# First rows of a mixture of experts by one-hot products, and its first weights loaded during the projection before it

## The chip, the cores and the metric

The kernel runs on one core of a Trainium2 chip. Five engines share its SBUF: TensorE (PE) multiplies matrices into PSUM, VectorE (DVE) and ScalarE (ACT) work elementwise, GpSimd (POOL) works elementwise and issues the indirect DMAs, SyncE (SP) issues most of the others. Sixteen DMA engines move data between HBM and SBUF. The metric is the device time of one execution in microseconds.

## The reference, cut to what matters

One sequence of 512 tokens of width 1024, fp32. A first block (a recurrent branch, an attention branch, a projection) gives h1; a hierarchical mixture of experts is added to it; a second block of two layers follows. The change is in the mixture and just ahead of it:

```python
mix = (ga * y_a + gb * y_b) @ w_out[l]
h = h + g1[:, None, :] * mix                      # h1
u2 = modulate(h, norm2_g[l], sh2, sc2)
# hier_moe: 4 groups x 8 experts, the best group, its two best experts for each token
g_sel = jnp.argmax(g_logits, axis=-1)
e_top, e_loc = lax.top_k(e_logits, 2)
gate = g_w * jax.nn.softmax(e_top, axis=-1)
hid = jax.nn.silu(xb @ w1[e]) * (xb @ w3[e])      # for the rows of expert e, D_EXPERT = 512
ys  = hid @ w2[e]
out = segment_sum(ys * row_gate, row_tok)
```

512 tokens with two experts each make 1024 assignments over 32 experts.

## The kernel before

**Around the change.** The weights of the first block stream through `wring`, five slots of 1 MB. SP loads a slot when PE has left it (`w_used`, L1401). The last projection (`out`) uses four slots, with homes 0 to 3, and the router's weights the one after, with home 4. Each slot takes 16 x 3 matmuls of PE. DVE adds each of eight results to x, which gives h1 (`h1_rdy`), and PE, ACT and DVE make the router's logits. ACT writes the normed rows to `u_tok` in SBUF and stores them to HBM as `u_rows` (`u_stored`).

**Routing.** DVE works out for each token its two experts, then (`ohot`) PE counts: `pos` is a token's place within its expert. From that DVE computes where each token goes: `tixI` is an index into a table in HBM, `destI` the row of its result. Each expert has a block of 64 rows, two experts are a pair, so a pair has 128 rows: 16 pairs, with spare blocks behind an `If` that is not taken here. POOL scatters the token numbers into the table (8 indirect DMAs, L1494), reads it back as `ids`, and for each pair gathers 128 rows of `u_rows` into `xs` (L1484). Rows of the table to which no token belongs hold 0, so row 0 is gathered for them. For pair 0 alone a shorter way is there: DVE makes a selection matrix `big` (L2018: token by row, 1 where the token is the j-th of expert 0 or 1), PE multiplies it by the token numbers (L2310), and the result `ids0` serves the first gather at once.

**The pairs.** `mring` has 12 parts of 1 MB on the bytes of `wring` and behind: for each of the pair's two experts a = 0, 1, four parts of w1 and w3 and two of w2, at places 6a + j. They cover homes 0 to 4 of `wring` (places 0 to 4), so a part cannot be loaded before its bytes are free. SP issues them in the order of its loop (L1419 for w1 and w3, L1428 for w2): all of pair 0 but the last two parts after h1 is complete, and from then on each part when its predecessor has been used (`used13`, `used2`). PE, for each pair: `gate_up` of expert 0, `down` of the previous pair's expert 1, `gate_up` of expert 1, the turning of the next pair's rows (`turn_x`, L2319), `down` of expert 0. In the first two pairs it also turns h1 to token rows (`h1_rows_turned`). DVE adds the shift to the turned rows (`x_turned`, L2076), which `gate_up` waits for. Results are stored to `y_rows`, gathered from there by `destI` (L1507) and added to h1.

**On PE ahead of pair 0**: count products, L2310, then `turn_x(0)`, then eight small products for `gate_row` (L2385), then pair 0. **On DVE**: the routing chain up to `destI` (L2048), block counts, `route_rdy`, then `x_turned(0)` (when the gather has landed and been turned), the gates, `gate_row`.

Of the kernel before, what the change touches and what calls it, by code (L numbers as in the profile page):

```python
# [31 lines left out]
MOE_ROWS = 64  # L32
MOE_PAIRS = EXPERTS // 2
# [43 lines left out]
def home(slot):  # L77

    return (slot + 1) % SLOTS
# [79 lines left out]
def build(nc, xT, crow, wmod, wrest, wfirst, wlayers, consts, vectors, brow, frow, lamv, rpb, w13, w2, out):  # L159
# [16 lines left out]
    with ExitStack() as ctx:  # L176

        def at(name, kb, shape, dt=F32):
            return nc.alloc_sbuf_tensor_at(name, shape, dt, offset=(nc.sbuf_base + 31) // 32 * 32 + int(kb * 1024))
# [50 lines left out]
        zeros = at("zeros", 116.5, [P, MOE_ALL + 1], I32)  # L230
# [40 lines left out]
        ids0 = at("ids0", 158.25, [P, 1], I32)  # L271
# [88 lines left out]
        shift_sum, shift_kept, picked, ids0_full, ids0_rdy = (sem(n) for n in ("shift_sum", "shift_kept", "picked", "ids0_full", "ids0_rdy"))  # L360
# [1024 lines left out]
        def _(sp):  # L1385
# [28 lines left out]
            def part13(p, a, src):  # L1414

                for j in range(4):
                    if not (isinstance(p, int) and p == 0):
                        sp.wait_ge(used13[a], 4 * p + j - 3)
                    sp.dma_start(mring[:, 6 * a + j, :], src(j)).then_inc(part_in[6 * a + j], 16)  # L1419

            def part2(p, a, src):

                for j in range(2):
                    if not (isinstance(p, int) and p == 0):
                        sp.wait_ge(used2[a], 2 * p + j - 1)
                    elif 6 * a + 4 + j == router:
                        sp.wait_ge(A.free, A_ROWS + 1)
# [40 lines left out]
        def _(pool):  # L1468
# [4 lines left out]
            pool.memset(zeros[:], 0).then_inc(pool_step, 1)  # L1473
            pool.wait_ge(pool_step, 1)
            pool.dma_start(table.rearrange("(p b) o -> p (b o)", p=P), zeros[:]).then_inc(table_clear, 16)
# [5 lines left out]
            def gather(p, rows):  # L1481
                if p >= 1:
# [28 lines left out]
            for p in range(1, MOE_PAIRS):  # L1511
                gather(p, ids[:, p:p + 1])
# [247 lines left out]
        def _(dve):  # L1760
# [246 lines left out]
            def chosen(to, by):  # L2007
# [8 lines left out]
            step(STT(out=q0, in0=b[:, 0:NQB * EXPERTS].rearrange("p (s e) -> p s e", e=EXPERTS)[:, :, 0:2], scalar=1.0, in1=M[:, :, 0:2], op0=ALU.add, op1=ALU.mult))  # L2016
            pick = big[:].rearrange("p (s a j) -> p s a j", s=NQB, a=2)
            TT(pick, K("block")[:, 1:].unsqueeze(1).unsqueeze(1).broadcast_to((P, NQB, 2, MOE_ROWS)),  # L2018
               q0.unsqueeze(3).broadcast_to((P, NQB, 2, MOE_ROWS)), ALU.is_equal).then_inc(picked, 1)
# [28 lines left out]
            step(dve.tensor_copy(destI[:], T("blk8")))  # L2048
            bb = big[:].rearrange("p (b e) -> p b e", e=EXPERTS)
# [22 lines left out]

            def x_turned(p):

                dve.wait_ge(xt_full, p + 1)
                dve.tensor_tensor(xT_[:], ps[:, 0:2, :].rearrange("p a (c n) -> p (a c) n", n=P),  # L2076
                                  mod[:, 24:32].unsqueeze(2).broadcast_to((P, DC, P)), ALU.add).then_inc(xt_done, 1)
# [46 lines left out]
            x_turned(0)  # L2124
# [60 lines left out]
        def _(pe):  # L2185
# [116 lines left out]

            pe.wait_ge(ohot, 1)
# [5 lines left out]
            for r in range(NQB):  # L2309
                ins = pe.matmul(ps[:, 7, 0:1], big[:, r * P:(r + 1) * P], K("token")[:, r:r + 1], start=(r == 0), stop=(r == NQB - 1))  # L2310
            ins.then_inc(ids0_full, 1)
            pe.wait_ge(A.free, A.made)
            pe.wait_ge(B.free, B.made)

            def turn_x(p):

                pe.wait_ge(xs_in, 16 * p + 16)
# [63 lines left out]
            turn_x(0)  # L2381
            pe.wait_ge(ids0_rdy, 1)
            for n in range(2):
                for c in range(4):
                    ins = pe.matmul(ps[n * 64:(n + 1) * 64, 7, c * P:(c + 1) * P], mod[:, 40 + 4 * n + c:41 + 4 * n + c].broadcast_to((P, 64)), ident,  # L2385
                                    start=True, stop=True)
            ins.then_inc(h1_turned, 1)
# [226 lines left out]
```

## Time and profile before

| what | value |
|---|---|
| median of 3 runs | 3367.93 us (3364.71 to 3369.0) |
| the profiled execution | 3363.76 us, span 3361.9 us |
| granted TensorE clock, mean | 0.973 of full |
| PE busy | 3045.0 us, 91% of the span |
| DVE, ACT, POOL busy | 1536.4, 988.9, 942.7 us |
| DMA | 465.80 MB, mean 139 GB/s |
| expert stage (first weight issue to last product) | about 641 to 1182 us |

Times in the trace are from the start of the span. The page divides the span into 40 slices of 84 us. A row of a timeline is a start, a duration (for merged instructions, of all of them), an engine, a line of the kernel, and in brackets how long the engine had been idle and what ended it. PEclk 1.00 is 2.4 GHz and 0.50 is 1.2 GHz. An fp32 matmul that is no transpose shows as two records.

### The profile page before, as it was taken

The page shows a single profiled execution, that of the slowest core. Times are in us where ns is not written, and L with a number is a line of the kernel's source. Part 1 is how long each engine was busy: PE and PEld are TensorE (multiplying, and loading weights), DVE is VectorE, ACT ScalarE, POOL GpSimd, SP SyncE. Part 2 cuts the span into 40 slices and gives each one's busy share as a digit, 9 for nine tenths or more (in the row PEclk, how much of TensorE's full clock was granted, in tenths as well). Part 3 has the DMA queues.
Part 4 walks back from the last instruction along what each step waited for, and adds up shares of the span by engine and source line. Part 5 has one row for each costly group of instructions (what it writes and reads, how often), then busy time and mean ns, then how long its engine had stood idle before and what let it go on. Part 6 is the DMA issues. An engine that isn't in the chain of part 4 may idle for free.

```text
span 3361.9 us, 32946 instructions
## 1 busy us (share of the span) xinstructions
PE 3045.0 (91%) x13112; PEld 2082.9 (62%) x13112; DVE 1536.4 (46%) x2562; ACT 988.9 (29%) x1398; POOL 942.7 (28%) x346
## 2 busy tenths in 40 slices
PE   3999998787777769999998899999999999889998
PEld 2777655632222247776745688887676755578886
DVE  7598856421111133645556622231645455742233
ACT  3653233200000043325243322223423434232222
POOL 2243102110000034332221344445432311244432
PEclk9999999999999979999999899999999999989999
DMA  5236312499999942121211122222121121122221
GB/s 226 88 113 239 112 50 80 168 367 422 422 422 422 421 156 74 67 76 52 87 50 38 63 100 100 90 99 95 50 88 63 63 75 38 50 76 93 95 100 50
DMA packets 71229, 465.80 MB, mean 139 GB/s; under 512 B 8785, under 2 KB 9073, under 8 KB 18993
## 3 DMA queue, kind: packets, MB, share of 16 engines
q1 hardware_dynamic: 60192, 436.31, 33.7%
q0 software_dynamic: 5200, 17.07, 1.4%
q10 hardware_dynamic: 5696, 10.49, 0.8%
q8 instruction: 95, 1.56, 0.2%
q14 instruction: 46, 0.37, 0.0%
HBM read 451.24 MB, written 12.60 MB: 138 GB/s over the span
## 4 chain that ended last, share of the span: by engine, by line
PE 75%; DMA 12%; DVE 8%; ACT 2%; issue 1%; POOL 0%; SPq 0%; ACTq 0%; DVEq 0%; POOLq 0%
PE ps L438 15%; PE ps L439 14%; PE ps L440 14%; DMA mring<-w 10%; PE ps L745 3%; PE ps L728 3%; PE ps L730 2%; PE ps L729 2%; PE ps L427 2%; PE ps L2256 2%; PE ps L908 2%; PE ps L760 1%; PE ps L2330 1%; PE ps L1014 1%; PE ps L973 1%
## 5 line engine op out<-in xcount | busy, mean ns | idle before, releaser
L497 POOL TENSOR_TENSOR w_lo<-wring,w_hi 128x2048 fp32r<-128x2048 f32 (+1 forms) x198 | 813.7, 4116 | 1729.6 <-ACT w_hi L487 1729.5
L438 PE MATMUL ps<-x_hi,w_hi 128*128 128x512 f32 (+1 forms) x1480 | 587.9, 397 | 18.2 <-ACT ps L1593 7.8
L440 PE MATMUL ps<-x_hi,w_lo 128*128 128x512 f32 (+1 forms) x1480 | 578.2, 391 | 0.0
L487 ACT ACTIVATE w_hi<-wring 128x2048 fp32r<-128x2048 f32 x176 | 336.0, 1911 | 315.9 <-PE ps L438 292.3
L439 PE MATMUL ps<-xf_lo,w_hi 128*128 128x512 f32 x1080 | 422.2, 391 | 0.0
L438 PEld LDWEIGHTS ps<-x_hi,w_hi 128*128 128x128 f32 (+1 forms) x1480 | 278.6, 188 | 90.4 <-ACT ps L1593 8.2
L440 PEld LDWEIGHTS ps<-x_hi,w_lo 128*128 128x128 f32 (+1 forms) x1480 | 278.5, 188 | 59.2
L2330 PE MATMUL ps<-mring,xT__95 128*64 128x512 f32 x512 | 242.6, 606 | 58.6 <-DMA mring<-w 54.6
L2331 PE MATMUL ps<-mring,xT__95 128*64 128x512 f32 x512 | 242.8, 606 | 0.0
L439 PEld LDWEIGHTS ps<-xf_lo,w_hi 128*128 128x128 f32 x1080 | 204.1, 189 | 41.7
L1368 DVE TENSOR_TENSOR g_f<-ps,g_f 128x512 f32<-128x512 f32 x44 | 30.4, 692 | 366.5 <-PE ps L440 350.0
L2330 PEld LDWEIGHTS ps<-mring,xT__95 128*64 128x64 f32 x512 | 63.9, 137 | 188.5 <-DMA mring<-w 123.8
L728 PE MATMUL ps<-x_hi,w_hi 128*128 128x512 f32 x336 | 159.0, 473 | 0.0
L1700 ACT ACTIVATE sil<-ps 64x512 f32<-64x512 f32 x32 | 19.0, 595 | 472.3 <-PE ps L2331 472.3
L2083 DVE TENSOR_TENSOR hid<-ps,sil 64x512 f32<-64x512 f32 x32 | 21.8, 682 | 296.3 <-ACT sil L1700 296.3
L439 PE MATMUL ps<-xa_lo,w_hi 128*128 128x512 f32 (+1 forms) x400 | 156.0, 390 | 0.0
L2349 PE MATMUL ps<-mring,hidT 128*64 128x512 f32 x512 | 116.9, 598 | 42.7 <-DVE hidT L2088 42.7
L1484 POOL DMA_INDIRECT xs<-u_rows,ids x16 | 15.2, 951 | 461.9 <-PE ps L2319 405.8
L438 PE MATMUL ps<-g_hi,w_hi 128*128 128x512 f32 x352 | 137.7, 391 | 0.0
L440 PE MATMUL ps<-g_hi,w_lo 128*128 128x512 f32 x352 | 137.0, 389 | 0.0
L439 PE MATMUL ps<-g_lo,w_hi 128*128 128x512 f32 x352 | 137.0, 389 | 0.0
L730 PE MATMUL ps<-x_hi,w_lo 128*128 128x512 f32 x336 | 132.7, 395 | 0.0
(520 smaller groups left out, 5468.1 us busy)
## 6 DMA issues: line engine op xcount, KB each, us to landing
mring<-w SPq DMA_DIRECT2D x192, 1024.0 KB, 28.4
wring<-wlayers SPq DMA_DIRECT2D x148, 1024.0 KB, 4.7
wring<-wfirst SPq DMA_DIRECT2D x44, 1024.0 KB, 4.8
mods<-wrest SPq DMA_DIRECT2D x16, 1024.0 KB, 4.7
wmodS<-wmod SPq DMA_DIRECT2D x4, 2048.0 KB, 18.2
y_rows<-ysb ACTq DMA_DIRECT2D x64, 128.0 KB, 6.5
rp<-rpb POOLq DMA_DIRECT2D x16, 192.0 KB, 2.6
hT<-xT SPq DMA_DIRECT2D x1, 2048.0 KB, 18.1
```

Of the source, the lines that this page charges most:

```text
L427: ins = pe.matmul(bank, w[:, 0:m], rhs[:, k, :], start=(k == 0), stop=(k == nk - 1))
L438: said(pe.matmul(bank, wh[:, 0:m], hi[:, k, :], start=(k == 0), stop=False))
L439: pe.matmul(bank, wh[:, 0:m], lo[:, k, :], start=False, stop=False)
L440: ins = pe.matmul(bank, wl[:, 0:m], hi[:, k, :], start=False, stop=(k == nk - 1))
L487: act.activation(w_hi[:, q % HI_SLOTS, :], wring[:, home(g), :], ACT.Copy).then_inc(hi_rdy, 1)
L497: ins = pool.tensor_tensor(w_lo[:, home(slot), o:o + n], wring[:, home(slot), o:o + n], w_hi[:, q % HI_SLOTS, o:o + n].bitcast(F32), ALU.s ...
L728: said(pe.matmul(state["bank"], wh, x[0][:, k, :], start=(k == 0), stop=False))
L730: ins = pe.matmul(state["bank"], wl, x[0][:, k, :], start=False, stop=(k == DC - 1))
L745: ins = pe.matmul(ps[:, 4 + k % 2, 0:u["nk"] * P], u["q"], u["k"], start=True, stop=True)
L2330: pe.matmul(ps[MOE_ROWS:P, 2 + a, :], x, w[:, 0:SEQ], start=(k == 0), stop=(k == DC - 1))
L2331: ins = pe.matmul(ps[0:MOE_ROWS, 2 + a, :], x, w[:, SEQ:D], start=(k == 0), stop=(k == DC - 1))
L2349: ins = pe.matmul(ps[n * MOE_ROWS:(n + 1) * MOE_ROWS, 5 + a, :], hidT[:, a, k, :], w[:, n * SEQ:(n + 1) * SEQ], start=(k == 0), stop=(k == 3))
```

## The change

1. Pair 0's rows are no longer gathered. PE multiplies `u_tok` by the selection matrix `big`, eight chunks by four token blocks, straight into the banks that `turn_x` writes; DVE's `x_turned(0)` follows right behind `destI`.
2. A second selection matrix, `big1`, gives pair 1's token numbers (`ids1`), with which the first gather is issued. It takes the place of `ids0`. Pairs 2 to 15 use `ids` as before.
3. The table is cleared to 2^20 in place of 0, and gathers have a bounds check, so that places without a token are skipped. Pair 1's `ids1` holds 0 for them.
4. SP issues parts (1,2) and (1,3) when the mix is complete, and (0,0), (0,1), (0,2) as PE leaves the slots of `out`. When h1 is complete it issues the other seven, (1,4) and (1,5) among them, which came behind the first reissues before.
5. The `gate_row` products move ahead of the count products on PE.

```diff
+            def first(a, j):
+                src = w13[a, j] if j < 4 else w2[a, j - 4]
+                sp.dma_start(mring[:, 6 * a + j, :], src).then_inc(part_in[6 * a + j], 16)
             assert router == 4
+            sp.wait_ge(mix2_rdy, DC)
+            first(1, 2)
+            first(1, 3)
+            for j in range(3):
+                slot = one["out"] // CHUNKS + j
+                sp.wait_ge(w_used, slot + 1)
+                first(0, j)
             sp.wait_ge(h1_rdy, DC)
-            for p in range(MOE_PAIRS):
+            for a, j in ((0, 3), (1, 0), (1, 1), (0, 5), (1, 4), (1, 5)):
+                first(a, j)
+            sp.wait_ge(A.free, A_ROWS + 1)
+            first(0, 4)
+            for p in range(1, MOE_PAIRS):
                 part13(p, 0, lambda j, e=2 * p: w13[e, j])
-                if p >= 1:
+                if p >= 2:
                     part2(p - 1, 1, lambda j, e=2 * p - 1: w2[e, j])
...
-            pool.memset(zeros[:], 0).then_inc(pool_step, 1)
+            pool.memset(none[:], NO_ROW).then_inc(pool_step, 1)
...
-                pool.indirect_dma_start(xs[:], None, u_rows, bass.IndirectOffsetOnAxis(ap=rows, axis=0)).then_inc(xs_in, 16)
+                pool.indirect_dma_start(xs[:], None, u_rows, bass.IndirectOffsetOnAxis(ap=rows, axis=0),
+                                        bounds_check=SEQ - 1, oob_is_err=False).then_inc(xs_in, 16)
-            pool.wait_ge(ids0_rdy, 1)
+            pool.wait_ge(ids1_rdy, 1)
             pool.wait_ge(u_stored, 16 * NQB)
-            gather(0, ids0[:, 0:1])
+            gather(1, ids1[:, 0:1])
...
+            pick(big, 0)
+            dve.wait_ge(picked, 1)
+            pick(big1, 1)
...
-            dve.wait_ge(ids0_full, 1)
-            dve.tensor_copy(ids0[:], ps[:, 7, 0:1]).then_inc(ids0_rdy, 1)
             whole(T("nb"), cts, MOE_ROWS, EXPERTS)
+            dve.wait_ge(ids1_full, 1)
+            dve.tensor_copy(ids1[:], ps[:, 6, 0:1]).then_inc(ids1_rdy, 1)
...
             step(dve.tensor_copy(destI[:], T("blk8")))
+            x_turned(0)
...
+            for n in range(2):
+                for c in range(4):
+                    ins = pe.matmul(ps[n * 64:(n + 1) * 64, 7, c * P:(c + 1) * P], ...)
+            ins.then_inc(h1_turned, 1)
             pe.wait_ge(ohot, 1)
...
             pe.wait_ge(picked, 1)
-            for r in range(NQB):
-                ins = pe.matmul(ps[:, 7, 0:1], big[:, r * P:(r + 1) * P], K("token")[:, r:r + 1], start=(r == 0), stop=(r == NQB - 1))
-            ins.then_inc(ids0_full, 1)
             pe.wait_ge(A.free, A.made)
+            for c in range(DC):
+                for r in range(NQB):
+                    ins = pe.matmul(ps[:, c // 4, (c % 4) * P:(c % 4 + 1) * P], u_tok[:, r, c * P:(c + 1) * P], big[:, r * P:(r + 1) * P],
+                                    start=(r == 0), stop=(r == NQB - 1))
+                if c == 1:
+                    pe.wait_ge(picked, 2)
+                    for r in range(NQB):
+                        row = pe.matmul(ps[:, 6, 0:1], big1[:, r * P:(r + 1) * P], K("token")[:, r:r + 1], start=(r == 0), stop=(r == NQB - 1))
+                    row.then_inc(ids1_full, 1)
+            ins.then_inc(xt_full, 1)
...
-            turn_x(0)
-            pe.wait_ge(ids0_rdy, 1)
```

## Rows read from the trace of the kernel before

**Rows 1.** The page, the 40 slices: what the DMA moved.

```profile
GB/s 226 88 113 239 112 50 80 168 367 422 422 422 422 421 156 74 67 76 52 87 50 38 63 100 100 90 99 95 50 88 63 63 75 38 50 76 93 95 100 50
```

**Rows 2.** Windows: length, busy time of the engines, PEclk, DMA share, GB/s.

```profile
606.00:640.00 34.00, 34.00 (x151) 27.93 (x149) 13.59 (x15) 10.42 (x15) 4.62 (x1) 1.00 0.00 0
641.00:672.00 31.00, 13.88 (x80) 8.96 (x76) 19.35 (x86) 10.59 (x15) 1.47 (x2) 0.75 0.98 394
672.00:684.00 12.00, 8.28 (x43) 6.63 (x45) 2.92 (x9) 1.59 (x3) 8.00 (x9) 0.66 0.28 87
684.00:1173.00 489.00, 383.04 (x1764) 129.54 (x1760) 74.65 (x116) 19.02 (x32) 14.72 (x16) 0.99 1.01 421
```

**Rows 3.** The chain that ended last: start, us, what.

```profile
655.20 14.20 DMA u_rows<-u_tok
...
688.83 12.05 DMA xs<-u_rows,ids
...
816.11 30.24 DMA mring<-w
```

**Rows 4.** Timeline of POOL, four gathers of one pair each.

```profile
731.07 0.94 POOL L1484 DMA_INDIRECT xs<-u_rows,ids  x1 [26.92 <-PE ps L2319]
757.73 0.94 POOL L1484 DMA_INDIRECT xs<-u_rows,ids  x1 [25.71 <-PE ps L2319]
...
817.27 0.94 POOL L1484 DMA_INDIRECT xs<-u_rows,ids  x1 [31.57 <-PE ps L2319]
849.63 0.94 POOL L1484 DMA_INDIRECT xs<-u_rows,ids  x1 [31.42 <-PE ps L2319]
```

**Rows 5.** Timeline of SP's queue, 560 to 700 us.

```profile
564.58 32.60 SPq L1401 DMA_DIRECT2D wring<-wfirst  x4
641.00 4.26 SPq L1419 DMA_DIRECT2D mring<-w  x8
...
682.74 4.86 SPq L1419 DMA_DIRECT2D mring<-w  x4
687.64 0.95 SPq L1428 DMA_DIRECT2D mring<-w  x2
```

**Rows 6.** Timeline of PE ahead of pair 0.

```profile
655.42 0.49 PE L2305 MATMUL ps<-gt,cs 128*128 128x128 f32 x2 [1.21 <-DVE gt L1994]
...
657.34 1.05 PE L2310 MATMUL ps<-cs,big 128*128 128x1 f32 x8 [1.06 <-DVE big L2018]
675.72 1.94 PE L2319 MATMUL ps<-cs,xs 128*128 128x128 f32 x8 [17.33 <-DMA xs<-u_rows,ids]
677.59 2.66 PE L2385 MATMUL ps<-cs,small 128*64 128x128 f32 x15
679.84 0.76 PE L2331 MATMUL ps<-mring,xT__95 128*64 128x512 f32 x1
```

**Rows 7.** Timeline of DVE, selection, destI and x_turned.

```profile
656.39 0.17 DVE L2016 SCALAR_TENSOR_TENSOR gt<-ps,gt 128x8 f32<-128x8 f32 x1
656.59 0.69 DVE L2018 TENSOR_TENSOR big<-cs,gt 128x512 f32<-128x512 f32 x1
...
665.21 0.17 DVE L2048 CAST destI<-gt 128x8 int32<-128x8 f32 x1
...
677.70 1.22 DVE L2076 TENSOR_TENSOR xT__95<-ps,small 128x1024 f32<-128x1024 f32 x1 [10.07 <-PE ps L2319]
```

**Rows 8.** Instructions of L2310: ns min/median/max, first and last start.

```profile
L2310 PEld LDWEIGHTS ps<-cs,big x8: 186/192/192, 657.3 to 658.1; 128*128 128x128 f32 x8
```

**Rows 9.** Windows of 1 us; PEclk is the third number from the end.

```profile
650.00:651.00 1.00, 0.98 (x5) 0.58 (x4) 0.86 (x5) 0.86 (x2) 0.00 (x0) 0.50 1.03 434
653.00:654.00 1.00, 0.83 (x8) 0.56 (x6) 0.90 (x5) 0.60 (x2) 0.00 (x0) 1.00 0.88 303
659.00:660.00 1.00, 0.00 (x0) 0.00 (x0) 0.83 (x5) 0.00 (x0) 0.00 (x0) 0.81 1.03 434
```

**Rows 10.** The chain that ended last, end of the expert stage.

```profile
1177.95 3.68 PE ps L2349 x16
```

More of the change, by code:

```diff
@@ L32 @@
 MOE_ROWS = 64
+NO_ROW = 1 << 20
 MOE_PAIRS = EXPERTS // 2
@@ L229, in build @@
         browS = sm(GROUPS + EXPERTS)[0:1, :]
-        zeros = at("zeros", 116.5, [P, MOE_ALL + 1], I32)
+        none = at("none", 116.5, [P, MOE_ALL + 1], I32)
         xr = at("xr", 96, [P, RC, SEQ + CONV_W])
@@ L270, in build @@
         ids = at("ids", 158, [P, MOE_ALL + 1], I32)
-        ids0 = at("ids0", 158.25, [P, 1], I32)
+        ids1 = at("ids1", 158.25, [P, 1], I32)
+        big1 = at("big1", 150, [P, NQB * P])
         shift_e = at("shift_e", 170.25, [P, 1])
@@ L1416, in part13 @@
                 for j in range(4):
-                    if not (isinstance(p, int) and p == 0):
-                        sp.wait_ge(used13[a], 4 * p + j - 3)
+                    sp.wait_ge(used13[a], 4 * p + j - 3)
                     sp.dma_start(mring[:, 6 * a + j, :], src(j)).then_inc(part_in[6 * a + j], 16)
@@ L1423, in part2 @@
                 for j in range(2):
[L1424 to L1427, printed above, removed]
+                    sp.wait_ge(used2[a], 2 * p + j - 1)
                     sp.dma_start(mring[:, 6 * a + 4 + j, :], src(j)).then_inc(part_in[6 * a + 4 + j], 16)
+            def first(a, j):
+                src = w13[a, j] if j < 4 else w2[a, j - 4]
+                sp.dma_start(mring[:, 6 * a + j, :], src).then_inc(part_in[6 * a + j], 16)
             assert router == 4
-            sp.wait_ge(h1_rdy, DC)
-            for p in range(MOE_PAIRS):
+            sp.wait_ge(mix2_rdy, DC)
[3 more added lines that the diff above has]
+                slot = one["out"] // CHUNKS + j
+                assert home(slot) == j
+                sp.wait_ge(w_used, slot + 1)
+                first(0, j)
+            sp.wait_ge(h1_rdy, DC)
+            for a, j in ((0, 3), (1, 0), (1, 1), (0, 5), (1, 4), (1, 5)):
[3 more added lines that the diff above has]
+            for p in range(1, MOE_PAIRS):
                 part13(p, 0, lambda j, e=2 * p: w13[e, j])
-                if p >= 1:
+                if p >= 2:
                     part2(p - 1, 1, lambda j, e=2 * p - 1: w2[e, j])
@@ L1472, in _ @@
             pool.memset(xr[:, :, 0:CONV_W - 1], 0.0).then_inc(pad_rdy, 1)
-            pool.memset(zeros[:], 0).then_inc(pool_step, 1)
+            pool.memset(none[:], NO_ROW).then_inc(pool_step, 1)
             pool.wait_ge(pool_step, 1)
-            pool.dma_start(table.rearrange("(p b) o -> p (b o)", p=P), zeros[:]).then_inc(table_clear, 16)
+            pool.dma_start(table.rearrange("(p b) o -> p (b o)", p=P), none[:]).then_inc(table_clear, 16)
             pool.dma_start(browS, brow).then_inc(brow_in, 16)
@@ L1510, in _ @@
             pool.dma_start(final_row[:], frow.partition_broadcast(P)).then_inc(row_in, 16)
-            for p in range(1, MOE_PAIRS):
+            for p in range(2, MOE_PAIRS):
                 gather(p, ids[:, p:p + 1])
@@ L2048, in _, with x_turned @@
             step(dve.tensor_copy(destI[:], T("blk8")))
+            def x_turned(p):
+                dve.wait_ge(xt_full, p + 1)
+                dve.tensor_tensor(xT_[:], ps[:, 0:2, :].rearrange("p a (c n) -> p (a c) n", n=P),
+                                  mod[:, 24:32].unsqueeze(2).broadcast_to((P, DC, P)), ALU.add).then_inc(xt_done, 1)
+            x_turned(0)
             bb = big[:].rearrange("p (b e) -> p b e", e=EXPERTS)
@@ L2122, in pair_dve @@
                     gated_out(p, 1)
-            x_turned(0)
             gates()
@@ L2301, in _ @@
                         rows_turned(r, n)
+            for n in range(2):
+                for c in range(4):
+                    ins = pe.matmul(ps[n * 64:(n + 1) * 64, 7, c * P:(c + 1) * P], mod[:, 40 + 4 * n + c:41 + 4 * n + c].broadcast_to((P, 64)), ident,
+                                    start=True, stop=True)
+            ins.then_inc(h1_turned, 1)
             pe.wait_ge(ohot, 1)
@@ L2379, in pair_pe @@
                     down(p, 1)
-            turn_x(0)
-            pe.wait_ge(ids0_rdy, 1)
[L2383 to L2387, printed above, removed]
             for p in range(2):
```

19 lines of the change are left out of this document (8 added, 11 removed).

## The prediction

> **What bounds the kernel now.** I read the page's forty slices first: in six neighbouring slices the DMA moves 421 to 422 GB/s, which nothing else in the kernel approaches [rows 1]. That is the expert stage. The windows give it exactly: over 684 to 1173 us the DMA engines are busy all the time at 421 GB/s, while PE is busy 383 of 489 us [rows 2]. The chain of waits says the same: each pair of experts costs one long wait for mring's weights [rows 3]. The starts of the gathers are a ruler for the pairs: 26.7 us apart while PE still works off weights that are already there, 32.3 us once the DMA sets the pace [rows 4]. Bytes explain 32.3: 12 weight parts of 1.0486 MB, 0.524 MB of gathered rows and 0.524 MB of stored y are 13.63 MB, at 422 GB/s 32.3 us.
>
> So the stage's end is the moment its byte stream ends, and that depends on three things: when the stream starts, the holes in it, and how many bytes it has. Ahead of 641.0 us, when h1 is complete and SP issues the first part, the DMA moves nothing for 34 us [rows 2, 5]. Between 672 and 684 us it moves 87 GB/s [rows 2]: ten parts are in, the next part needs a buffer that pair 0 frees, and pair 0 starts at 679.84 us [rows 6]. SP issues the next part at 682.74 us [rows 5]. Why so late? The chain: u_rows is stored behind ten queued parts (14.20 us), then POOL gathers pair 0's rows from it, PE turns them at 675.72, and DVE adds the shift [rows 3, 6, 7].
>
> **The change, term by term.**
>
> Term A, pair 0 starts earlier. Its x comes from 32 one-hot matmuls on u_tok, which is in SBUF already, instead of store, gather and turning. Two chains must end. DVE: destI was written by 665.38 [rows 7]. Ahead of it come the second selection (as the first, 0.20 and 0.69 us with a wait of 0.1 [rows 7]: 1.0 us) and some delay because PE now does the eight gate-row matmuls before the count matmuls; 16 records at 0.11 us are 1.8 us in a wait that was 1.2 us [rows 6], so 0.6 us. DVE is free at 667.0. PE: an fp32 matmul shows as two records; with a 128x128 weight tile at the full clock they start 0.114 us apart (eight between 657.3 and 658.1 [rows 8]). The one-hots are 64 records and the token numbers of pair 1 another 8: 72 x 0.114 = 8.2 us. Picked comes at 657.28 + 0.6, so PE ends at 666.1, with the latency of the last one 666.4. At the low clock a record costs 0.23 us (eight turning records in the 1.87 us ahead of L2385 [rows 6]), and then PE ends at 674.5. Which? PEclk was 0.50 in 650 to 651 with PE fully busy, 1.00 again in 653 to 654, and fell once more in 659 to 660, after thin work [rows 9]. I expect the same second fall, for about 3 us, since the work before it is nearly as thin: 13 records lost, 1.5 us. PE ends at 667.9, x_turned takes 1.22 us [rows 7], pair 0 starts at 669.5 instead of 679.84: **10.3 us**. Bounds: full clock, where DVE decides, 668.4 (11.4 us); low clock throughout 675.9 (3.9 us). The page FP8 and Floating Point Precision of the Trainium skill (section TensorE Precision Notes) says true fp32 takes four passes of the array: 128 columns x 4 at 2.4 GHz would be 0.213 us a matmul where the rows show 0.228, and A would be 0.4 us more. The rows' value stands.
>
> What waits on this edit? DVE's copy of ids1 comes behind the products of two chunks and the token numbers, 24 records, done at 661.1, when DVE has got there (659.67 + 1.6 = 661.3 for the end of the first `whole`); at the low clock it is 2 us late, which the PE chain then covers. On DVE the block counts, gates and gate_row now come behind x_turned, 4.5 us of small operations up to about 673; PE wants gate_row copied when it turns h1 near 677, and ACT and DVE want their results later still. POOL's gather for pair 1 now waits only for ids1 (about 661) and u_stored, which comes sooner as 7 parts instead of 10 lie ahead, about 664. Then eight table scatters of 1.3 us run from about 667 to 677. Pair 1 is turned some 17 us after pair 0 starts, near 687, so the 3.3 us in which PE waited for that gather (landing 12.05 us after its issue [rows 3]) vanish. That is hidden: PE is ahead of the DMA from then on anyway.
>
> Term B, the early parts. The last projection's four weight slots take PE from about 597.2, when the last wfirst load could be issued [rows 5], to 640.5; a quarter is 10.8 us. So two parts go at about 599 and one each at 608, 619 and 630, and all five have landed by 635, in DMA time that was empty [rows 2]. At 641 seven follow, where before ten did; parts (1,4) and (1,5), issued before at 687.64 [rows 5] behind the hole, now go ahead of it. So two parts, 2.10 MB, leave the bound stream. The other three only make the hole longer: 7 parts and 2.10 MB of u_rows need about 22 us, so the DMA is idle from about 665 to 673. It loses nothing that A does not already count. SP's new waits block nothing: behind them stand only these loads. PE runs at full pace in the projection while wfirst loads land, and I give the early loads no price.
>
> Term C, fewer gathered bytes. 1024 assignments fill half of 16 x 128 rows. Pairs 2 to 15 now skip theirs: 14 x 64 rows x 4 KB = 3.67 MB. Pair 1's gather (0.52 MB; its ids come from a product, empty rows read row 0) moves into the hole, so it leaves the stream too. No row shows a gather with skipped rows; between nothing and all 3.67 MB I take all, since the DMA is byte-bound in rows 2.
>
> B and C: 2.10 + 3.67 + 0.52 = 6.29 MB at 422 GB/s are 5.0 + 8.7 + 1.2 = **14.9 us**. The page DMA: Bandwidth & Descriptors of the Trainium skill (Specifications) puts HBM at about 358 GB/s a core; by that these bytes were 17.6 us. This trace reads at 422, so 14.9.
>
> Is the stream whole after it resumes? It resumes 4 us after pair 0 starts. Eight parts freed by both first products last it to 24 us, final_row (0.52 MB) and the gather of pair 2 to 26 us; down frees the next at about 23 us. No new hole; at worst 2 us. The tail (last down at 1177.95 [rows 10], y stored, gathered, normalised) hangs on the end of the stream and moves whole. The second block is unchanged.
>
> Sum: 10.3 + 14.9 = 25.2 us. The profiled execution took 3363.8 (span 3361.9), so 3338.6; the median of the runs is 4.2 us higher, so **3343 us**.
>
> **Rivals.** (1) Skipped rows save nothing, because the time goes by descriptors or by 128 places whatever their size: 8.7 us less gain, 3351 us. For it: no row shows such a gather. Against: the 32.3 us fits bytes to a tenth. (2) The one-hot products run at the low clock throughout and pair 0 starts at 675.9: gain 18.8, 3349 us. For it: the clock fell at 659 [rows 9], when PE fell idle; against: PE is now busy, as in 650 to 653, when it came back in 3 us. (3) Slower: the bounds check makes the gather slow on POOL. It is issued when a pair has been turned and needed one pair later. Of 31.7 us, the 12 us to landing leave about 19 us beyond its 0.94 us [rows 4]. From 20 us of issue time it would decide; the 25 us are gone at 21.8 us (1.8 us in each of 14 pairs), and at 23 us each pair takes 3.3 us longer than forecast, which makes 3389 us. POOL does nothing else then; every indirect issue here took about 1 us. (4) The change does nothing measurable: the next limit sits just below the DMA. PE's 27 us a pair against 31.7 speaks against it; it needs A, B and C each to fail, about 3368 us.
>
> **How the numbers follow.** Forecast 0.65; rival 1 0.15; rival 2 0.12 (both together 3358); rival 3 0.03; rival 4 0.05. The upper end takes in rivals 1 and 2: 3355. The lower: A at its best gives 1.1, the first reissue may come 0.9 us sooner at the full clock, runs differ by 4 us: 3337. A change within 0.2% (6.7 us) cannot be told from none here. Faster 0.93, same 0.04, slower 0.03.
>
> **What would show it.** In the changed profile: five mring issues before 636 us and seven after 641; pair 0's first L2331-type matmul at 669 to 670 us; SP's next part at about 672; gathers 31.7 us apart in the middle of the stage instead of 32.3; the last down at about 1152.8 instead of 1177.95. If the pairs stay at 32.3 us, C is wrong; if the one-hot records start 0.23 us apart, A is. A DMA hole after the resumption, a late gather, or w_lo or the projection's matmuls slowed by the early loads would make the sum wrong.

## The result and the profile after

The changed kernel takes 3345.43 us (median of 4 runs, 3343.75 to 3347.56) against 3367.99 (4 runs of the kernel before beside it): ratio 0.9939 [0.9925, 0.9953], 22.6 us faster. The profiled execution took 3345.81 us, span 3344.0. In it the load of xS, ahead of the last projection's weights, is 2.03 us later than in the profile of before (566.24 and 564.21), so places are compared by their distance from that load. Over all profiles of this document it lies between 563.86 and 569.53: that much comes from the part of the kernel that nobody changed, and it blurs the whole times. For the whole block I use one length, **the stage**: from that load to POOL's first gather of y. It was 626.56 us and is 605.29: 21.3 us less. A second profile of the changed kernel gives 604.39, so two stages that differ by under 1 us are not told apart. A **reissue** is a part that SP loads into a place of `mring` that an earlier pair has used.

SP's queue; it answers to [rows 5]:

```profile
566.24 0.33 SPq L1402 DMA_DIRECT2D xS<-xT  x1
566.61 32.60 SPq L1403 DMA_DIRECT2D wring<-wfirst  x4
601.29 47.92 SPq L1431 DMA_DIRECT2D mring<-w  x12
671.65 15.26 SPq L1420 DMA_DIRECT2D mring<-w  x8
```

The twelve first parts are issued from 601.3 to 649.2, five of them during the projection. The first reissue is at 671.65, 105.4 us after xS; before it was 118.5. That is 13.1 us earlier.

PE ahead of pair 0 and the pace of the one-hot products, answering to [rows 6] and [rows 8]:

```profile
655.66 1.58 PE L2328 MATMUL ps<-cs,small 128*64 128x128 f32 x16
657.44 0.49 PE L2333 MATMUL ps<-gt,cs 128*128 128x128 f32 x2 [0.20 <-DVE gt L2010]
...
659.36 2.05 PE L2340 MATMUL ps<-big,u_tok 128*128 128x128 f32 x16 [1.06 <-DVE big L2037]
661.25 0.95 PE L2345 MATMUL ps<-cs,big 128*128 128x1 f32 x8
662.06 5.60 PE L2340 MATMUL ps<-big,u_tok 128*128 128x128 f32 x48
669.68 0.61 PE L2365 MATMUL ps<-mring,xT__96 128*64 128x512 f32 x1 [2.02 <-issue]
```

```profile
L2340 PE MATMUL ps<-big,u_tok x64: 275/275/377, 659.4 to 667.4; 128*128 128x128 f32 x64
```

DVE's chain beside it, to compare with [rows 7]:

```profile
667.67 0.17 DVE L2068 CAST tixI<-gt 128x8 int32<-128x8 f32 x1
...
668.15 0.17 DVE L2071 CAST destI<-gt 128x8 int32<-128x8 f32 x1
668.36 1.23 DVE L2075 TENSOR_TENSOR xT__96<-ps,small 128x1024 f32<-128x1024 f32 x1
```

The products end at 667.7; DVE is busy with the routing until 668.32, then adds the shift, and pair 0 starts at 669.68, 103.4 us after xS (115.6 before). So DVE's chain decides, by 0.6 us.

The clock at the places of [rows 9]; PEclk is the third number from the end:

```profile
650.00:651.00 1.00, 1.00 (x9) 0.96 (x10) 0.53 (x4) 0.05 (x1) 0.00 (x0) 1.00 0.99 418
653.00:654.00 1.00, 1.00 (x8) 0.66 (x7) 0.86 (x5) 0.60 (x2) 0.00 (x0) 1.00 0.96 385
659.00:660.00 1.00, 0.64 (x5) 0.64 (x6) 0.93 (x3) 0.00 (x0) 0.00 (x0) 1.00 1.06 442
```

In this profile it never left 2.4 GHz here. That is not the same in every execution: in the second profile of the changed kernel it fell to 1.2 GHz for 3 us ahead of the one-hot products, as it did before in 650 to 653, with PE busy in both. What is gone in both profiles of the changed kernel is the long low stretch of before that begins when PE falls idle at 659. First before, then the second profile of the changed kernel (its load of xS is at 569.53):

```profile
660.00:672.00 12.00, 0.00 (x0) 0.00 (x0) 6.63 (x31) 0.00 (x0) 1.47 (x2) 0.50 1.02 425
```

```profile
656.00:658.00 2.00, 1.88 (x8) 1.57 (x8) 1.72 (x9) 1.33 (x3) 0.00 (x0) 0.50 1.01 389
660.00:670.00 10.00, 8.94 (x82) 8.66 (x81) 8.67 (x37) 1.77 (x2) 0.00 (x0) 1.00 1.01 416
```

The DMA, in windows around the restart of the weights, to set beside [rows 2]:

```profile
668.00:673.70 5.70, 4.01 (x20) 1.74 (x22) 4.20 (x15) 0.80 (x3) 2.59 (x3) 1.00 0.26 57
670.00:672.00 2.00, 2.00 (x12) 0.84 (x10) 1.52 (x6) 0.00 (x0) 1.19 (x2) 1.00 0.00 0
...
676.00:678.00 2.00, 1.36 (x8) 0.42 (x4) 0.47 (x1) 0.59 (x1) 1.70 (x2) 1.00 1.01 410
678.00:680.00 2.00, 1.13 (x8) 0.68 (x10) 1.25 (x3) 0.00 (x0) 1.39 (x3) 1.00 1.31 336
680.00:685.00 5.00, 5.00 (x26) 1.66 (x24) 0.26 (x1) 0.00 (x0) 1.57 (x2) 1.00 1.02 289
685.00:690.00 5.00, 4.10 (x28) 2.43 (x24) 2.71 (x4) 0.59 (x1) 0.19 (x1) 1.00 0.88 202
690.00:700.00 10.00, 9.32 (x44) 3.21 (x46) 1.32 (x3) 0.00 (x0) 2.04 (x3) 1.00 1.00 422
```

This is the part to read slowly. The engines show full (share 1.31, 1.02, 0.88), but bytes move at 336, 289 and 202 GB/s. POOL's timeline says what else is under way:

```profile
670.51 1.10 POOL L1499 DMA_INDIRECT xs<-u_rows,ids  x1 [54.08 <-DMA u_rows<-u_tok]
671.91 1.04 POOL L1510 DMA_INDIRECT table<-tokI,tixI  x1 [0.30 <-issue]
...
680.91 0.97 POOL L1510 DMA_INDIRECT table<-tokI,tixI  x1 [0.30 <-issue]
689.81 0.60 POOL L1513 DMA_DIRECT2D ids<-table  x1 [7.94 <-DMA table<-tokI,tixI]
695.46 0.56 POOL L1526 DMA_DIRECT2D final_row<-frow  x1 [5.05 <-DMA ids<-table]
```

The eight table scatters lie beside the weights now. After the last issue POOL waits 7.94 us for them; before, the same wait was 1.47:

```profile
680.57 0.97 POOL L1494 DMA_INDIRECT table<-tokI,tixI  x1 [0.30 <-issue]
683.01 0.59 POOL L1497 DMA_DIRECT2D ids<-table  x1 [1.47 <-DMA table<-tokI,tixI]
```

The gathers deep in the stage, as [rows 4] were for before:

```profile
803.46 0.99 POOL L1499 DMA_INDIRECT xs<-u_rows,ids  x1 [30.96 <-PE ps L2354]
835.75 0.99 POOL L1499 DMA_INDIRECT xs<-u_rows,ids  x1 [31.30 <-PE ps L2354]
867.47 0.99 POOL L1499 DMA_INDIRECT xs<-u_rows,ids  x1 [30.73 <-PE ps L2354]
```

The last nine intervals (pairs 6 to 14) have a mean of 31.87 us, **the period** from here on; before it was 32.28. They are not alike: 32.29, 31.72, 31.69, 32.00, 32.12, 31.70, 31.90, 31.71, 31.72. The last `down` of the chain, against [rows 10]:

```profile
1120.25 30.00 DMA mring<-w
...
1158.83 3.73 PE ps L2384 x16
```

### The profile page after: what moved, and what is told of

It is laid out like the page before. It is cut to its first block, busy times and chain, and to the rows that moved or that the text cites. A ratio compares the mean times of both kernels' runs of the same rounds, so it can differ in the third digit from the quotient of the medians.

```text
span 3344.0 us, 33075 instructions
## 1 busy us (share of the span) xinstructions
PE 3049.2 (91%) x13168; PEld 2086.3 (62%) x13168; DVE 1535.4 (46%) x2564; ACT 987.9 (30%) x1398; POOL 940.5 (28%) x345
## 3 DMA queue, kind: packets, MB, share of 16 engines
q0 software_dynamic: 5056, 12.82, 1.2%
## 4 chain that ended last, share of the span: by engine, by line
PE 75%; DMA 12%; DVE 8%; ACT 2%; issue 1%; SPq 0%; POOL 0%; ACTq 0%; DVEq 0%; POOLq 0%
PE ps L440 15%; PE ps L442 14%; PE ps L441 14%; DMA mring<-w 11%; PE ps L747 3%; PE ps L730 3%; PE ps L731 2%; PE ps L732 2%; PE ps L429 2%; PE ps L2279 2%; PE ps L910 2%; PE ps L762 1%; PE ps L2365 1%; PE ps L1016 1%; PE ps L975 1%
## 5 line engine op out<-in xcount | busy, mean ns | idle before, releaser
L731 PE MATMUL ps<-xa_lo,w_hi 128*128 128x512 f32 x336 | 132.7, 395 | 0.0
```

Source lines behind the costliest of these rows:

```text
L731: pe.matmul(state["bank"], wh, x[1][:, k, :], start=False, stop=False)
```

## The experiments

All but the fifth are edits of the changed kernel. Median, ratio to the kernel before run beside them, stage and period (stage and period from one profile each). Many of the ratios' intervals overlap with that of the changed kernel, those of 1, 2, 4, 7 and 9 among them; what is said of these rests on the stage and on the windows of the traces:

| kernel | us | ratio [95%] | stage | period |
|---|---|---|---|---|
| before | 3367.99 | 1 | 626.56 | 32.28 |
| changed | 3345.43 | 0.9939 [0.9925, 0.9953] | 605.29 | 31.87 |
| 1 gathers full | 3351.51 | 0.9952 [0.9939, 0.9964] | 611.53 | 32.30 |
| 2 no early parts | 3353.85 | 0.9959 [0.9946, 0.9972] | 613.36 | 31.93 |
| 3 no scatters | 3336.16 | 0.9906 [0.9893, 0.9919] | 599.27 | 31.72 |
| 4 scatters twice | 3353.45 | 0.9962 [0.9949, 0.9975] | 613.11 | 31.93 |
| 5 before, skipping | 3361.52 | 0.9983 [0.9974, 0.9992] | 619.54 | 31.91 |
| 6 only the one-hots | 3359.64 | 0.9984 [0.9975, 0.9993] | 619.71 | 32.31 |
| 7 rows first | 3341.07 | 0.9932 [0.9919, 0.9946] | 603.53 | 31.87 |
| 8 all skipped | 3327.81 | 0.9889 [0.9873, 0.9904] | 590.00 | 31.16 |
| 9 ids by products | 3340.66 | 0.9918 [0.9905, 0.9932] | 600.38 | 31.93 |
| 10 uneven rows | 3350.15 (one run) | | 606.92 | 32.27 |
| 11 one expert's rows | 3343.5 (one run) | | 606.75 | 32.28 |
| changed, again | 3348.38 | 0.9934 [0.9921, 0.9948] | 604.39 | 31.91 |

### 1. Gathers full

```diff
-            pool.memset(none[:], NO_ROW).then_inc(pool_step, 1)
+            pool.memset(none[:], 0).then_inc(pool_step, 1)
...
-                pool.indirect_dma_start(xs[:], None, u_rows, bass.IndirectOffsetOnAxis(ap=rows, axis=0),
-                                        bounds_check=SEQ - 1, oob_is_err=False).then_inc(xs_in, 16)
+                pool.indirect_dma_start(xs[:], None, u_rows, bass.IndirectOffsetOnAxis(ap=rows, axis=0)).then_inc(xs_in, 16)
```

> The changed kernel, but the table is cleared to 0 and the gathers have no bounds check, so every gather moves all 128 rows. By the prediction's term C (a skipped row costs nothing) the pairs are 32.28 us apart again in place of 31.87, and the whole is 8.7 us slower than the changed kernel. By the reading of its trace (gathers 31.87 us apart, 0.23 more than the bytes ask for, and 896 more packets under 512 B) a skipped row is not free: 14 x 0.41 = 5.8 us slower. If skipping does nothing at all: 0.

The stage grows by 6.2 us and the period returns to 32.30. Skipping does save time, so rival 1 falls, but it saves 0.43 us a pair where the bytes alone give 8.7 / 14 = 0.62.

### 2. No early parts

```diff
-            sp.wait_ge(mix2_rdy, DC)
-            first(1, 2)
-            first(1, 3)
-            for j in range(3):
...
             sp.wait_ge(h1_rdy, DC)
-            for a, j in ((0, 3), (1, 0), (1, 1), (0, 5), (1, 4), (1, 5)):
+            for a, j in ((0, 0), (0, 1), (0, 2), (0, 3), (1, 0), (1, 1), (1, 2), (1, 3), (0, 5), (1, 4), (1, 5)):
                 first(a, j)
```

> The changed kernel with its five early parts issued with the other seven when h1 is complete. The 12.4 us that they take then fill the DMA's hole of 668 to 673.7 first: by the prediction (the three parts of the hole gain nothing, two gain 5.0 us) 5 to 7 us slower than the changed kernel. Pair 0 still starts near 670, with its four parts in place. Rival: the early loads are what lets pair 0 start, 12 us slower. Other rival: all is hidden, 0.

8.1 us longer, above the 5 to 7 expected. All twelve parts now go at 646.13 and later, and the DMA is never empty before the reissue at 675.00. Five parts back in the stream are 12.4 us; the thin stretch of the changed kernel that they fill (668 to 673.7, at 57 GB/s) takes 4.9 of these off again, which leaves 7.5. The rest may be the scatters, all of which now lie beside the weights. This prices the five parts together; no run moves the two parts of term B alone.

### 3. No scatters

Pairs 2 to 15 use a fixed table, token 5 in places 0 to 31 and 64 to 95 and none in the others, and the eight scatters are gone. The routing of these pairs is left out.

```diff
-            for k in range(2):
-                for r in range(NQB):
-                    c = k * NQB + r
-                    pool.indirect_dma_start(table, bass.IndirectOffsetOnAxis(ap=tixI[:, c:c + 1], axis=0),
-                                            tokI[:, r:r + 1], None).then_inc(table_set, 16)
-            pool.wait_ge(table_set, 16 * 2 * NQB)
```

> The changed kernel without the eight table scatters; the table holds a fixed pattern, 64 of 128 places with a row, so every later gather is as large as before (the routing of pairs 2 to 15 is left out). Theory of the collision: in the changed kernel the scatters run from 672 to 690 us beside the resumed weight stream, which moves 294 GB/s in 674 to 690 instead of 422, 4.7 us lost; without them the stream is at 400 or more there and the kernel 4 to 5 us faster than the changed one. Rival: the stream is thin there since PE frees the parts of pair 0 too slowly (no collision): same time, and still about 300 GB/s.

6.0 us less in the stage. The low windows are gone:

```profile
676.00:680.00 4.00, 2.49 (x16) 1.12 (x12) 1.28 (x2) 0.59 (x1) 0.55 (x1) 1.00 0.99 410
680.00:684.00 4.00, 4.00 (x20) 1.35 (x20) 0.69 (x1) 0.00 (x0) 0.00 (x0) 1.00 1.02 421
684.00:688.00 4.00, 4.00 (x24) 1.74 (x21) 0.06 (x1) 0.60 (x1) 0.00 (x0) 1.00 1.01 423
```

Not all 6.0 are the scatters': its period is 0.15 shorter, which over 14 pairs may be up to 2.1 us of it. Experiments 10 and 11 get round this.

### 4. Scatters twice

A second set of the same eight scatters goes to another table that nobody reads.

```diff
+                    pool.indirect_dma_start(table2, bass.IndirectOffsetOnAxis(ap=tixI[:, c:c + 1], axis=0),
+                                            tokI[:, r:r + 1], None).then_inc(table_set, 16)
-            pool.wait_ge(table_set, 16 * 2 * NQB)
+            pool.wait_ge(table_set, 16 * 4 * NQB)
```

> The changed kernel with the eight scatters done a second time, into a table that nobody reads. Theory of the collision: another 4 to 5 us are lost on the stream, the kernel is that much slower, with a low rate up to about 700 us; if the gather of pair 2, which comes behind, is then late, PE waits for it near 716 us, but PE is ahead of the stream. Rival (the stream is thin for want of freed parts): no change in the rate and at most 1 us.

7.8 us more, at the same period (31.93). The stream stays low until the last write is in:

```profile
672.00:676.00 4.00, 3.01 (x16) 1.11 (x12) 1.30 (x3) 0.74 (x2) 3.07 (x4) 1.00 1.00 407
...
684.00:688.00 4.00, 1.65 (x14) 1.29 (x12) 0.00 (x0) 0.00 (x0) 3.08 (x4) 1.00 0.94 183
688.00:692.00 4.00, 0.00 (x0) 0.00 (x0) 0.00 (x0) 0.00 (x0) 1.29 (x2) 0.85 1.06 160
```

The engines are busy all the while (0.94, 1.06) at 183 and 160 GB/s. Not all of the 7.8 us is surely the scatters': in this one profile ACT starts an instruction at 692.25 after 17.2 us of waiting for something that the trace does not name, PE stands still for 8.6 us behind it, and the DMA share falls to 0.72 in 696 to 700 us, about 1 us of idle DMA:

```profile
692.25 0.59 ACT L1722 ACTIVATE sil<-ps 64x512 f32<-64x512 f32 x1 [17.20 <-remote]
694.28 1.12 PE L2399 MATMUL ps<-cs,hT 128*128 128x128 f32 x4 [8.63 <-DVE h_tok L2130]
```

Two directions, taking a set away and adding one, give a price of the same order for 1024 writes of 4 bytes: 6.0 (less what the period gives) and up to 7.8 us.

### 5. The kernel before, skipping

```diff
-            pool.memset(zeros[:], 0).then_inc(pool_step, 1)
+            pool.memset(zeros[:], 1 << 20).then_inc(pool_step, 1)
...
-                pool.indirect_dma_start(xs[:], None, u_rows, bass.IndirectOffsetOnAxis(ap=rows, axis=0)).then_inc(xs_in, 16)
+                pool.indirect_dma_start(xs[:], None, u_rows, bass.IndirectOffsetOnAxis(ap=rows, axis=0),
+                                        bounds_check=SEQ - 1, oob_is_err=False).then_inc(xs_in, 16)
```

> The kernel before with the cleared table at 2^20 and the bounds check alone. Its scatters run in the hole of 672 to 683 and stay free. From the pairs' spacing (32.28 against 31.87 us) 15 x 0.41 = 6.2 us faster than before; by the prediction's term C 15 x 0.62 = 9.3 us. If skipping does nothing: 0.

Its stage is 7.0 us shorter, with 15 gathers that skip where experiment 1 has 14, and its period is 31.91: in a pair the skipping is worth the same without the rest of the change. Its scatters stay in the hole, and POOL's wait for them is 1.47 us, as in before.

### 6. Only the one-hot products

Full gathers, and SP's loop as before.

```diff
-            sp.wait_ge(mix2_rdy, DC)
-            first(1, 2)
-            first(1, 3)
...
-            for p in range(1, MOE_PAIRS):
+            for p in range(MOE_PAIRS):
                 part13(p, 0, lambda j, e=2 * p: w13[e, j])
-                if p >= 2:
+                if p >= 1:
```

> The changed kernel with full gathers and with the order of loads of the kernel before (ten parts when h1 is complete, none early): the one-hot products and the gather of pair 1 by ids1 alone. Ten parts and u_rows keep the DMA busy to about 674, and pair 0 frees parts from about 671: no hole, where the kernel before had one of 10.3 us, and one gather less, 1.2 us. By the prediction's sum 11 us faster than before. By the theory of the collision the scatters, which lay in that hole, now take 6 us of the stream: only 5 to 6 us faster than before.

6.9 us, where pair 0 starts 11.9 us earlier (103.69 us after xS). The hole is closed, and the scatters (672.7 to 682.6) lie beside the weights; POOL's wait for them is 8.60 us. The one-hot products alone bring on the cost. Experiments 6 and 1 also split the gain in three: one-hots 6.9 us (626.56 to 619.71), early parts 8.2 (to 611.53), skipping 6.2 (to 605.29).

### 7. Rows first

The last four first parts wait until `u_tok` has been read for `u_rows`.

```diff
-            for a, j in ((0, 3), (1, 0), (1, 1), (0, 5), (1, 4), (1, 5)):
+            for a, j in ((0, 3), (1, 0), (1, 1)):
+                first(a, j)
+            sp.wait_ge(A.free, A_ROWS + 1 + 2 * NQB)
+            for a, j in ((0, 5), (0, 4), (1, 4), (1, 5)):
                 first(a, j)
-            sp.wait_ge(A.free, A_ROWS + 1)
-            first(0, 4)
```

> The changed kernel, but SP issues only three of the seven parts when h1 is complete and the other four when all rows of u_tok are made, so that u_rows is stored ahead of them. The gather of pair 1 then goes at about 663 in place of 670.5 (times of the changed kernel's trace) and the scatters start when their indices are there, at 668, in place of 671.9: 5.6 us of their 10.3 us lie in the DMA's hole (668 to 673.7) in place of 1.8. By the theory of the collision (6.0 us lost by eight scatters in the stream) about 2 to 2.5 us faster than the changed kernel. Rival (the price is paid per scatter wherever it lies, or the four parts are late): 0 or slower by 1 to 2.

The gather goes at 663.28, the scatters from 666.25 to 676.6, and the stage is 1.8 us shorter (0.9 against the second profile of the changed kernel), where 2 to 2.5 had been expected. By the whole time this is not told apart (0.9932 and 0.9939, with intervals of 0.0014 to either side). POOL's first scatter now waits 1.87 us for DVE's tokI, so the routing chain is what stops it from going sooner still.

### 8. All skipped

As 3, with no token in any place of pairs 2 to 15.

> The changed kernel without the scatters and with a table of nothing but 2^20, so that the gathers of pairs 2 to 15 skip all 128 rows (their routing and rows are left out). In e3_no_scatter half the rows were skipped and the pairs were 31.72 us apart. Bytes alone ask for 31.04. If a skipped row costs nothing: 31.0 to 31.1. If it costs a third of a fetched one: about 31.45. If the gather's fixed price is the larger part: above 31.6. In the whole 14 x 0.65 = 9 us faster than e3_no_scatter in the first case.

From pair 9 on the intervals are 31.08 to 31.12 us. The other 13.11 MB of a pair at 422 GB/s are 31.06: 128 skipped places cost under 0.1 us. From 3 to 8, 64 rows are 0.56 to 0.63 us, and their bytes 0.62. So a skipped place is free; something else held back a third of the saving in the real routing, where the number of rows is half as well.

### 9. Ids by products

Each pair's token numbers come from a selection matrix and four small products, two pairs ahead, as pair 1's do. Token numbers are shifted by 1024, so that an empty place gives 1024 and is skipped. Table and scatters move into the `If` that is not taken. It computes all that the changed kernel does.

```diff
+                if ahead:
+                    next_pick(p + 2)
...
+            def row_ids(p, bank):
+                pe.wait_ge(picked, p + 1)
+                pe.wait_ge(ids1_rdy, p - 1)
+                for r in range(NQB):
+                    row = pe.matmul(ps[:, bank, 0:1], big1[:, r * P:(r + 1) * P], tokm[:, r:r + 1], start=(r == 0), stop=(r == NQB - 1))
+                row.then_inc(ids1_full, 1)
```

> A version for use: no table scatter on the path that is taken. The row numbers of pairs 2 and 3 are made in pair 0 and those of pair p + 2 in pair p, by the selection and the four small products that the changed kernel has for pair 1 (about 0.9 us of DVE and 0.9 us of PE a pair); the table, its scatters and its reading back stand behind the test for overflow. By the theory of the collision it gains what e3_no_scatter gained, 6.0 us against the changed kernel, counted from the load of xS to the first gather of y_tok (599.3 in place of 605.3), and about 3339 us in all. Rival: the products and waits put into PE's and DVE's order make a pair longer than the stream's 31.9 us, or thin the stream while PE sets the pace: then less, or slower.

3340.66 (3336.98 to 3341.07) against 3348.38 (3340.03 to 3349.27) for the changed kernel beside it; the intervals of the two ratios overlap. The stage is 600.38, 4.0 and 4.9 us less than in the two profiles of the changed kernel. The stream is whole:

```profile
674.00:690.00 16.00, 13.90 (x80) 6.70 (x76) 6.48 (x13) 1.76 (x3) 0.32 (x1) 1.00 1.00 405
804.00:1090.00 286.00, 226.17 (x1076) 78.09 (x1074) 48.16 (x90) 10.68 (x18) 8.90 (x9) 1.00 1.02 422
```

405 GB/s where the changed kernel had 294 in the same 16 us; at 422 GB/s the difference is 4.2 us of stream, about what the stage gained. What it adds, 0.5 us of PE and 0.9 us of DVE in a pair (226.17 against 221.68 us and 48.16 against 40.02 over nine pairs), is hidden: the period is 31.93. Of the versions that do the whole work it has the lowest median, level with 7.

### 10. Uneven rows

64 rows in a pair again (token 5 in each), but in the places with p mod 16 < 8. Scatters and routing of pairs 2 to 15 are left out as in 3, and the table is not read back either.

```diff
+            step(dve.reduce_sum(T("bq")[:, 0:8], ident.rearrange("p (a b) -> p a b", b=16)[:, :, 0:8], AX_X))
+            step(dve.reduce_sum(T("bq")[:, 8:9], T("bq")[:, 0:8], AX_X))
+            TS(ids[:], T("bq")[:, 8:9].broadcast_to((P, MOE_ALL + 1)), -float(NO_ROW), float(NO_ROW + 5), ALU.mult, ALU.add).then_inc(ids_in, 1)
```

> The changed kernel without scatters, its row numbers written by DVE: of 128 places those with p mod 16 under 8 hold a row, the other half is skipped (routing of pairs 2 to 15 left out). As many rows as in e3_no_scatter, whose places 0 to 31 and 64 to 95 gave 31.72 us a pair. If a gather's time is that of the fullest of the 16 DMA engines and neighbouring places go to different engines (e3 says they cannot go eight in a row to one, or it would have stayed at 32.3), these rows sit on eight engines and the pairs are up to 32.3 us apart, as if nothing were skipped. If only the bytes count: 31.7.

32.27 us a pair: with half of the bytes it takes what the full gather takes (32.30). The bytes do not set the time of a gather; how they fall on the sixteen DMA engines does. Which places share an engine it leaves open: two layouts fit 3 and 10 alike.

### 11. One expert's rows

As 3, with token 5 in places 0 to 63 and none in 64 to 127. The diff is against experiment 3.

```diff
-            for h in range(2):
-                pool.memset(none[64 * h:64 * h + 32, :], 5).then_inc(pool_step, 1)
-            pool.wait_ge(pool_step, 3)
+            pool.memset(none[0:64, :], 5).then_inc(pool_step, 1)
+            pool.wait_ge(pool_step, 2)
```

> The kernel without scatters again, with another fixed table for pairs 2 to 15: places 0 to 63 of each pair hold a token, places 64 to 127 none. The routing of these pairs is left out, so this is a time of 64 valid places in a pair, as in the kernel without scatters (places 0 to 31 and 64 to 95, 31.72 us a pair) and in the one with places p mod 16 < 8 (32.27 us). What it tells apart is which places share a DMA engine. If neighbouring places go to different engines (engine = place mod 16), every engine gets 4 rows a pair here: 31.72 us a pair, first weight of the block to first gather of y about 599.3 us, and my estimate for the real routing by the fullest engine would be 0.53 us less a pair over pairs 6 to 14. The Trainium skill, page DMA: Bandwidth & Descriptors, section The descriptor swizzle, gives engine = 8 * (place >> 6) + ((place >> 2) & 7) for a transfer to 128 partitions: then engines 0 to 7 get all 64 rows, 8 each, as many as in a full gather. By that rule worked out as a mechanism of this kernel: 32.27 us a pair, as the uneven table gave, 14 x 0.55 = 7.7 us more than without scatters, stage about 607 us; and with the real routing the fullest engine (8) would have 50 of 72 possible rows over pairs 6 to 14, 22 x 16 rows of 4 KB less at 422 GB/s = 0.38 us a pair, where 0.43 and 0.37 us were measured. I expect the latter, 0.8.

```profile
1057.73 0.99 POOL L1501 DMA_INDIRECT xs<-u_rows,ids  x1 [31.31 <-PE ps L2350]
1090.02 0.99 POOL L1501 DMA_INDIRECT xs<-u_rows,ids  x1 [31.30 <-PE ps L2350]
```

32.28 us: one half of the places is served by one half of the engines. Places dealt to engines one after the other would have given 31.72.

Experiments 10 and 11 also price the scatters without the period's share that clouds experiment 3: they have the period of experiment 1 (32.27, 32.28 and 32.30) and no scatters, and their stages are 606.92 and 606.75 where experiment 1 has 611.53. The 4.6 and 4.8 us are the scatters'. In the 16 us behind the restart experiment 11 moves 414 GB/s, experiment 1 at the same place 283, each in one profile:

```profile
672.60:688.60 16.00, 13.84 (x75) 6.06 (x70) 5.50 (x11) 2.02 (x3) 1.51 (x2) 1.00 1.01 414
```

```profile
676.70:692.70 16.00, 13.87 (x76) 6.09 (x72) 5.59 (x11) 1.97 (x3) 5.82 (x7) 1.00 0.99 283
```

### The changed kernel again

> The changed kernel once more, beside e9_ids_by_products on one chip: about 3345 us, 605.3 us from the load of xS to the first gather of y_tok.

Stage 604.39, period 31.91, and the same uneven intervals in the same places (32.29, 31.76, 31.69, 32.09, 32.21, 31.77, 31.96, 31.73, 31.71). The unevenness belongs to the routing and is no noise. In experiment 7, with the same routing, it falls on other pairs (31.79, 31.71, 31.85, 32.30, 32.05, 31.69, 31.71, 32.02, 31.70), at the same mean.

## Why the prediction came out right, and where its steps did not

The forecast was 3343 us, a gain of 25.2; the medians show 22.6 and the stage 21.3. Two terms missed by about as much in opposite directions, and that they cancel is luck; one cost, put at nothing, makes up nearly all of the rest.

**The bound and its three levers** were read rightly: start, holes and bytes of the stream account for nearly all of the 21.3 us.

**Term A, 10.3 us, was too small.** Pair 0 starts 12.2 us earlier and the first reissue is 13.1 us earlier. The expected second fall of the clock did not come: through the one-hot products PEclk was 1.00 in both profiles of the changed kernel and in those of experiments 1, 2 and 6, with PE busy there and not idle as before. The first fall comes and goes between profiles of the same order of work, and costs pair 0 under 0.3 us (103.71 us after xS with it, 103.44 without). What remains is the full-clock bound of the prediction, with DVE deciding, as it said (destI 668.32 and 1.23 us); it had given 11.4, and up to 0.9 more for the reissue. Rival 2 did not occur.

**Term B, 5.0 us,** has its issue order right: (1,4) and (1,5) lie ahead of the first reissue. By itself it is not measured. All five early parts are worth 8.1 us (experiment 2) or 8.2 (from experiment 6 to 1); that is more than 5.0 because the thin stretch they leave behind is shorter than forecast, 668 to 673.7 (by the time of before 666 to 671.7) where 665 to 673 was said, and this surplus is the one already counted in A.

**Term C, 8.7 us of skipped rows, was too large:** 6.2 us by experiment 1, 7.0 by experiment 5. Its bytes are right: queue 0 moves 12.82 MB, 16.55 in experiment 1, and the difference of 3.73 MB is close to the 3.67 that was said. "Because the DMA is byte-bound" is where it fails. A pair's rows come in two blocks of 64 places, filled from the front, and a thin end of a block leaves some engines idle while others have their full eight rows. The Trainium skill (DMA: Bandwidth & Descriptors, The descriptor swizzle) gives the engine as 8 * (place >> 6) + ((place >> 2) & 7); experiments 3, 10 and 11 agree with it (31.72, 32.27 and 32.28 us for a fullest engine of 4, 8 and 8 rows), and 11 excludes place mod 16. With the tokens of each expert counted from the reference's inputs, the fullest engine would by that rule carry 50 of 72 rows over pairs 6 to 14, an estimate of 22 x 65.5 KB of 16-engine time at 422 GB/s, 3.4 us or 0.38 a pair. Measured by the periods: 0.43 and 0.39 (changed, twice, against experiment 1) and 0.38 (experiment 5 against before). The pairs bear it out one by one: by the same rule and counts engine 8 gets 8, 4, 4, 8, 8, 4, 6, 4 and 4 rows in pairs 6 to 14, and the intervals of the changed kernel are 32.29, 31.72, 31.69, 32.00, 32.12, 31.70, 31.90, 31.71 and 31.72. The intervals of experiment 7 go rather with engine 0 (4, 4, 5, 8, 4, 4, 4, 8, 4 rows), so which engine is behind can differ. Open is the rest over the whole stage: engine 8 is spared 31 rows in pairs 2 to 15, an estimate of 4.8 us, where experiment 1 measures 6.2.

**The step that failed: "No new hole; at worst 2 us", with the eight scatters costed at nothing.** Before, they ran in the 12 us in which the DMA was nearly empty [rows 2], and POOL waited only 1.47 us for them. Term A closes just that hole. The prediction did place them, from 667 to 677 us and so across the restart of the weights, and gave them no price there. They came later still, from 671.9, because `u_rows` was stored later than forecast: pair 1's gather went at 670.51, by the time of before 668.5, where 664 was said. Beside the weights they hold the stream at 294 GB/s for 16 us. Five comparisons bear on it: against the full gathers with the same period 4.6 and 4.8 us less without them (10 and 11); 6.0 us less in 3, up to 2.1 of it from the even table; up to 7.8 more with a second set (4); the one-hots alone give 6.9 instead of some 11 (6); and replaced by products with the real routing 4.0 to 4.9 less (9). I take 4 to 5 us.

Together: 25.2 + 2.8 (A) - 2.5 (C) - 4 to 5 (scatters) = 20.5 to 21.5, where the stage gave 21.3. What a scatter does to the engines that makes its 4 bytes so dear is not shown. Before had dips of its own in 684 to 700 us, 386 GB/s in place of 422 or 1.4 us; no run tests them. Rival 3 is excluded by gather issues of 0.99 us, rival 4 by the result.

**The signs.** Right: five issues of mring from 601.3 to 631.5 and seven from 643.0 to 649.2. Pair 0 at 669.68 and the reissue at 671.65 meet the forecast (669.5 and about 672) by luck: this execution was 2.03 us late at the load of xS, and by their distance from it both come 2 us and more earlier than forecast. Wrong: 31.87 for 31.7, by what stands above, and the last `down` at 1158.83 for 1152.8, by that and by the same 2.03 us.

## What to carry to other kernels

A hole in the stream that bounds a stage is not empty because its bytes are few: before closing it, list every DMA that runs in it, and price each beside the stream instead of in the hole. A gather that skips rows saves by its fullest DMA engine and not by its bytes, so valid rows should be spread over the places that different engines serve (experiments 3 and 11: 31.72 and 32.28 us for the same bytes). Small writes into HBM can be replaced by a product on an engine with time to spare (experiment 9). Moving them to where the stream is idle is the other way, of which experiment 7 shows 0.9 to 1.8 us.

## What the runs showed of the hardware

- 1024 indirect writes of 4 bytes beside a saturated load stream cost 4 to 5 us of it (experiments 9, 10 and 11), a second set up to 7.8 (experiment 4). An estimate from this: 4.7 us x 16 engines / 1024 is 0.07 us of an engine for each, 0.12 by the second set. The engines' share stayed at 0.94 to 1.06 while bytes fell to 160 GB/s. Whether they are free in an empty DMA no run tests; the kernel before, where they ran at 5 to 230 GB/s, waited 1.47 us for the last of them. The Trainium skill says that DMAs of all issuing engines run on the same 16 engines and interleave (DMA: Bandwidth & Descriptors, Issuing engines are not separate DMA queues), which these windows agree with.
- A gathered row that the bounds check skips costs nothing that shows: 128 of them in a pair leave 31.08 to 31.12 us where the other bytes alone need 31.06.
- The same 0.262 MB of gathered rows take a pair to 31.72 or to 32.28 us by which of the 128 places they go to.
- PEclk stayed at 1.00 through 641 to 700 us in one profile of the changed kernel and was 0.50 in 656 to 658 in the other, with PE busy 1.88 of those 2 us. Before, it was at 0.50 in 660 to 672, with PE idle.
